# Moving the first head's rough scores, row maxima and shift row into the projection's last tile, with early table loads

## The reference, cut to what matters

```python
u = rmsnorm(h, g_attn)
proj = u @ w_in                      # fox q | k | v | forget logits | MLA q-latent | MLA kv-latent + rope key
fq = rmsnorm(to_heads(fq, 8), g_fox_q); fk = rmsnorm(to_heads(fk, 8), g_fox_k)
cum = cumsum(log_sigmoid(ff + b_f))
logits = (fq @ fk.T) / 8 + cum[query] - cum[key]      # causal, 8 heads of 64 ("fox")
o_fox = softmax(logits) @ fv
# then: MLA (8 heads, low-rank q and kv), output projection, residual,
# and a mixture of 32 experts (top 1 of 4 groups, top 2 of its 8 experts)
```

## Time and profile before

| what | us |
|---|---|
| median of 3 runs | 628.41 (627.26 to 628.76) |
| the profiled execution's own time | 628.14 |
| its span, from the first to the last instruction | 626.4 |
| PE busy | 587.5 (94% of the span) |
| PEld, DVE, ACT, POOL busy | 408.1, 265.6, 233.8, 140.9 |
| mean granted TensorE clock | 0.988 of full speed |

### The profile page before, as it was taken

One profiled execution on the slowest core, in us unless ns is written; L12 is line 12 of the kernel. 1 busy time (PEld: TensorE's weight loads), 2 busy tenths in 40 slices (PEclk: granted clock), 3 DMA queues, 4 the chain that ended last, 5 costly groups with the idle time before them and its releaser, 6 DMA issues.

```text
span 626.4 us, 9256 instructions
## 1 busy us (share of the span) xinstructions
PE 587.5 (94%) x3559; PEld 408.1 (65%) x3559; DVE 265.6 (42%) x603; ACT 233.8 (37%) x445; POOL 140.9 (22%) x233
## 2 busy tenths in 40 slices
PE   8899999998999989999989999999999997877896
PEld 8778788786775447666778766566566554554554
DVE  3644245554484988437745771111111111101217
ACT  6826516543555473456616522212122121111220
POOL 6300001150233412122510011332322322212200
PEclk9999799999999989999989999999999999999999
DMA  8930000006400053000199499999999999999995
GB/s 274 335 121 1 0 2 0 1 2 239 182 1 0 34 235 135 10 1 1 30 427 413 146 412 370 372 397 379 395 393 384 389 398 393 394 395 391 398 378 216
DMA packets 32941, 141.64 MB, mean 226 GB/s; under 512 B 8689, under 2 KB 10785, under 8 KB 19841
## 3 DMA queue, kind: packets, MB, share of 16 engines
q1 hardware_dynamic: 26016, 127.02, 52.3%
q0 software_dynamic: 6304, 11.93, 5.8%
q10 hardware_dynamic: 576, 2.10, 0.8%
HBM read 132.85 MB, written 16.06 MB: 238 GB/s over the span
## 4 chain that ended last, share of the span: by engine, by line
PE 82%; DVE 10%; issue 4%; ACT 3%; POOL 1%; DVEq 0%; ACTq 0%; POOLq 0%
PE ps L2314 18%; PE ps L1953 16%; PE ps L2345 10%; PE ps L2149 6%; PE ps L2272 5%; PE ps L2032 4%; PE ps L2138 3%; PE ps L2087 3%; PE ps L2330 2%; PE ps L2107 2%; PE ps L1917 2%; DVE sums_s L1703 1%; PE ps L1926 1%; DVE x L1864 1%; PE ps L2193 1%
## 5 line engine op out<-in xcount | busy, mean ns | idle before, releaser
L2314 PE MATMUL ps<-w,xt 128*64 128x256 f32 x1024 | 116.6, 380 | 15.3 <-issue 15.0
L2314 PEld LDWEIGHTS ps<-w,xt 128*64 128x64 f32 x1024 | 76.9, 137 | 61.7 <-issue 33.0
L1633 DVE TENSOR_TENSOR xt<-ps,g_ffn_c 128x512 f32<-128x512 f32 x32 | 22.0, 692 | 187.1 <-PE ps L2272 187.1
L2345 PE MATMUL ps<-w,hT 128*64 128x512 f32 x256 | 61.8, 604 | 0.0
L1290 ACT ACTIVATE hsb<-ps,row_scale 128x256 f32<-128x256 f32 x32 | 15.2, 475 | 113.8 <-PE ps L2314 113.8
L917 POOL DMA_INDIRECT xg<-h_rows,idx x30 | 28.8, 960 | 109.0 <-PE ps L2272 108.6
L909 POOL DMA_INDIRECT y_rows<-yh,idy x29 | 29.5, 1016 | 65.3 <-ACT yh L1312 62.4
L2149 PE MATMUL ps<-probT,vals 128*128 128x512 f32 (+4 forms) x160 | 42.7, 411 | 1.0 <-POOL probT L846 1.0
L1714 DVE TENSOR_REDUCE nmax<-ps 128x1 bf16<-128x528 f32 (+1 forms) x64 | 28.0, 502 | 35.9 <-PE ps L2108 35.9
L846 POOL TENSOR_SCALAR_AFFINE_SELECT probT<-probT 128x128 f32<-128x128 f32 (+2 forms) x80 | 21.2, 288 | 83.8 <-ACT probT L1202 82.5
L2272 PEld LDWEIGHTS ps<-ident,xg 64*128 64x128 f32 x256 | 30.2, 200 | 11.6 <-issue 11.5
(11 more groups left out here) (353 smaller groups left out, 1061.8 us busy)
## 6 DMA issues: line engine op xcount, KB each, us to landing
w<-in_w SPq DMA_DIRECT2D x96, 1024.0 KB
x<-in_x SPq DMA_DIRECT2D x8, 512.0 KB, 9.5
y_rows<-zeros POOLq DMA_DIRECT2D x1, 4096.0 KB, 12.3
yg<-y_rows SPq DMA_DIRECT2D x4, 1024.0 KB, 11.0
w_in_v<-in_w_in SPq DMA_DIRECT2D x1, 2048.0 KB, 11.0
w_in_k<-in_w_in SPq DMA_DIRECT2D x1, 2048.0 KB, 16.8
w_in_q<-in_w_in SPq DMA_DIRECT2D x1, 2048.0 KB, 21.6
w_oa<-in_w_o SPq DMA_DIRECT2D x1, 2048.0 KB, 10.2
```

Of the source, the lines that this page charges most:

```text
L2314: ins = pe.matmul(ps[j * slots:(j + 1) * slots, 2 + b, 0:F], xt[b][:, k, :], w13[s][:, j, k, :], start=(k == 0), stop=(k == DK - 1))
L2345: ins = pe.matmul(ps[q * slots:(q + 1) * slots, 6 + b, :], hT[b][:, m, :], w2s[s][:, m, q * 512:(q + 1) * 512], start=(m == 0), stop=(m == ...
```

## The change

1. `max_scores` gets the head as an argument: head 0's rough scores go to PSUM banks 0, 1 and 5 and those of all others to 3, 4 and 5, as before.
2. PE: `score_maxes(0)` stands ahead of the projection of the last unit (ckv, tile 3), behind waits for all turned heads' copies, for `narrowed`, the masks, and the units that held banks 0 and 1. `turn_row(0)` stands ahead of the last turn. The fillers there are 7 in place of 14, in another bank. In `attend(0)` both calls are gone, and so are the 3 + 3 fillers; `attend(1)` keeps its own calls and its 2 fillers.
3. DVE: `row_maxes(0)` stands in the projection's loop, at the last unit but one (ckv, tile 2), behind the copy out of tile 1's turn. `attend(1)` keeps its own call for head 8.
4. ACT: behind `shift_row` of heads 0 and 8 a one-column exp is added, and behind `up_square(0)` a call of `load_root_table`.

```diff
-        def max_scores(i):
+        def max_scores(g, i):
             n = query_keys(i)
+            b0 = 0 if g == 0 else 3
             if i == 3:
-                return pair(3, n)
-            bank, c0 = {2: (4, META), 1: (5, 0), 0: (5, query_keys(1))}[i]
+                return pair(b0, n)
+            bank, c0 = {2: (b0 + 1, META), 1: (5, 0), 0: (5, query_keys(1))}[i]
             return ps[:, bank, c0:c0 + n]
...
                 shift_row(g0)
+                act.activation(junk[:, 0:1], eps_c[:, :], ACT.Exp)
                 for g in range(g0, g0 + H):
...
                     if g == H - 1:
                         up_square(0)
+                        load_root_table()
                         up_root(0)
...
+            def row_maxes(g):
+                for n, i in enumerate(MAX_ORDER):
+                    dve.wait_ge(max_scored, 2 * g + n // 2 + 1)
+                    dve.tensor_reduce(nmax[g % 2][:, i:i + 1], max_scores(g, i), X, ALU.max, negate=True
+                                      ).then_inc(maxed, 1)
...
                 if n >= 1 and units[n - 1] in stage_no and not by_act(units[n - 1]):
                     empty_turn(units[n - 1])
+                if n == len(units) - 2:
+                    row_maxes(0)
...
-                row_maxes(g0)
                 if ph == 1:
+                    row_maxes(g0)
                     add_fox(1)
                 row_maxes(g0 + 1)
...
+            def score_maxes(g):
+                h = g % H
+                for n, i in enumerate(MAX_ORDER):
+                    if h and n in (0, 2):
+                        pe.wait_ge(maxed, NT * (g - 1) + n + 2)
+                    keys, to = query_keys(i), max_scores(g, i)
...
+            def turn_row(g):
+                pe.wait_ge(maxed, NT * (g + 1))
+                if g % H:
+                    pe.wait_ge(row_out, g)
...
             for what, u in steps:
+                if what == "project" and u == units[-1]:
+                    pe.wait_ge(turn_act, sum(by_act(v) for v in turns))
+                    pe.wait_ge(turn_low, sum(by_act(v) for v in turns))
+                    pe.wait_ge(narrowed, sum(by_act(v) for v in turns))
+                    pe.wait_ge(masks_made, 15)
+                    unit_emptied(pe, len(units) - 4)
+                    unit_emptied(pe, len(units) - 3)
+                    score_maxes(0)
...
                 if u == steps[-1][1] and what == "turn":
-                    unit_emptied(pe, len(units) - 4)
-                    keep_warm((len(units) - 4) % 4, 14)
+                    turn_row(0)
+                    unit_emptied(pe, len(units) - 2)
+                    keep_warm((len(units) - 2) % 4, 7)
                 turn(u) if what == "turn" else project(u)
...
-                score_maxes(g0)
                 if ph == 1:
+                    score_maxes(g0)
                     out_project(1, 0, 1)
                 score_maxes(g0 + 1)
-                keep_warm(OUT, 0 if ph else 3)
-                turn_row(g0)
-                keep_warm(OUT, 2 if ph else 3)
                 if ph == 1:
+                    turn_row(g0)
+                    keep_warm(OUT, 2)
                     pe.wait_ge(fox_added, 2)
```

More of the change, by code:

```diff
@@ L1981, in gather @@
                 pe.matmul(dst, side, part[b][:, 0:w], start=True, stop=True).then_inc(projected, 1)
-            for what, u in steps:
+            def score_maxes(g):
[4 more added lines that the diff above has]
+                    keys, to = query_keys(i), max_scores(g, i)
+                    q = qTb[0:depth(g), h, i * P:(i + 1) * P]
+                    for c0 in range(0, keys, 512):
+                        c1 = min(keys, c0 + 512)
+                        m0 = max(c0, keys - P)
+                        pe.matmul(to[:, c0:c1], q, kTb[0:depth(g), h, c0:c1], start=True, stop=False)
+                        ins = pe.matmul(to[:, m0:c1], identb[:, :],
+                                        causal[:, m0 - (keys - P):c1 - (keys - P)], start=False, stop=True)
+                    if n in (1, 3):
+                        ins.then_inc(max_scored, 1)
+            def turn_row(g):
+                pe.wait_ge(maxed, NT * (g + 1))
+                if g % H:
+                    pe.wait_ge(row_out, g)
+                for i in range(NT):
+                    ins = pe.matmul(ps[0:1, ROW, i * P:(i + 1) * P], nmax[g % 2][:, i:i + 1], identb[:, :],
+                                    start=True, stop=True)
+                ins.then_inc(row_turned, 1)
+            for what, u in steps:
+                if what == "project" and u == units[-1]:
[6 more added lines that the diff above has]
+                    score_maxes(0)
                 if what == "spread":
@@ L2093, in attend @@
                 g0 = ph * H
[L2095 to L2121, removed]
                 def score(g):
```

## The result

| what | before | after |
|---|---|---|
| median us (runs) | 627.33 (7; 626.17 to 628.76) | 623.44 (7; 622.70 to 624.56) |
| profiled execution's own time | 628.14 | 622.70 |
| its span | 626.4 | 621.1 |
| mean granted clock | 0.988 | 0.982 |

The ratio is 0.9937, 95% interval 0.9919 to 0.9954: 3.9 us faster, where 3.5 were forecast. Against the 628.41 of the first three runs 624.9 had been forecast; over seven runs the kernel before stands 1.1 us lower. The two profiled executions differ by 5.4 us, more than the medians, and most of this document is about which part of that is the change.

The account below looks back on a forecast made before the run. PE was taken to bound the kernel (82% of the chain), with DMA of weights setting the late end but passing the gain on. Seam -3.72 and root +0.20 gave -3.52, from 628.41 to 624.9 us, range 623.7 to 626.3.

Parts of the forecast that it names:

- The seam: Between projection and fox attention: exact scores start at 150.90 to 150.92 in place of 154.64, 3.72 us less.
- Maxima, row, copy: Head 0's maxima (1.75 us), row (0.31) and ACT's copy (0.58) delay nothing; head 1's row is covered by 0.2 us.
- Tables: Added one-column activations on ACT move no table load; at the root 0.20 us more, perhaps 0.10.
- The sum: Seam and root together: -3.72 + 0.20 = -3.52 us, median 624.9 us.
- Rival (a): With thirteen of twenty fillers gone the clock falls at the seam, costing 1.7 to 3.5 us: 626.6 to 628.4; chance 0.07.
- Rival (b): The clock's fall at the seam lasts into the fox heads: 630.3 us or more; chance 0.03.
- (c): Table loads wait with their activations, so the added ones pull them forward, up to 1.28 - 0.20 gained: 623.6; chance 0.04.
- (d): The gain is lost behind fox attention, as weights' stream or another transfer keeps the end: about 627.5 to 628.6; chance 0.06.

Follow-up runs that it names:

- the move alone: The changed kernel without the added one-column activations; 623.45 us, ratio 0.9931 to the kernel before.
- the trimmed one: The kernel before with 8 fillers for 14 ahead of the last turn and none around head 0's row, nothing moved; 629.49 us, ratio 1.0030.
- the tables alone: The kernel before with only the added one-column activations (exp, root); 627.84 us, ratio 0.9997.
- the delay: The changed kernel with 17 more fillers ahead of the second head's rough scores; 627.41 us, ratio 0.9999 to the kernel before.

## Why the prediction was right

- *The seam.* Forecast 3.72, measured 3.65 along the chain. Rough scores 0.85 for 0.95, the last unit 3.27 for 3.19, the second head's rough scores 7.55 behind the turn of tile 1 for 7.47: the list of waits ahead of `attend(0)`, with a wait more in it, took 0.45 where 0.34 had been read. The last turn was put at 148.61 on the clock of before; it came 6.22 us behind the end of tile 1's turn, which is 148.65.
- *Maxima, row, copy.* As forecast: no one waited for them. The second head's row was the nearest thing to a stop: score(0) ends at 153.58 and the row starts there, 0.06 behind the last maximum (151.77 + 1.75 = 153.52), where 0.2 of cover had been forecast; score(0) took 1.55 and not 1.70.
- *Tables.* Direction right, size halved: 0.09 us on the path and not 0.20. The step that was off is the price of a back-to-back start, taken at the full 202 ns of the earlier trace rows where 0.10 had been named beside it.
- *The sum.* -3.65 + 0.09 gives -3.56. The medians moved by 3.9 with an interval of 2.9 to 5.1, so nothing beyond the sum is shown. The profiled pair differed by 5.3 of span: by the table +1.04 ahead of the seam, -3.76 at it, +0.04 in the heads, +0.09 by the root, -1.05 in the MLA stage, -1.66 behind the last copy. The three that are neither seam nor root go with where each execution happened to meet the low clock; the forecast, made on one trace, had no term for that. In the medians nothing of them can be told.
- *Rival (a), the clock.* It didn't happen, so the 0.07 wasn't tested by the result; the experiments say that the reasoning for so low a chance was too light. It leaned on one trace of before in which a seam with two gaps kept 1.00. That seam was kept by its fillers: with six fewer (8 + 3 + 3) the clock fell in the trace, and by their times in most runs, and the new seam without its seven took 626.72 in the median, 3.3 us more than the move alone on the same chip. The price (half of the low stretch, 1.7 to 3.5 us) was right: 3.03 measured. The Trainium skill, "TensorE: Matmul & The Clock Gate", section "A second HAM failure mode: psum-queue depth-cycling", had said that short idles between groups of matmuls can let the clock swing; the second trace without fillers agrees, at 0.50 behind 4 us in which PE worked 1.5, and the first, with the same work and 1.00, shows that it need not.
- *Rival (b), slower.* The same mechanism did make a kernel slower than before, the trimmed one (+2.2 us, ratio 1.0030): its low stretch was about 10 us and its seam only 0.7 shorter, where the forecast, for a seam 3.5 us shorter, had the break-even at 7 us and a loss of over 0.3% at 10.8. So it was a real rival in kind.
- *Rivals (c) and (d)* fell by the tables alone and by the delay.

## What to carry to other kernels

Work that one phase needs first (here rough scores, maxima and the row of its first head) can often be put among the last steps of the phase ahead, where it needs only banks that are free by then; what it takes there is hidden as long as the last copy of that phase sets the seam. Filler matmuls on the chain are not slack until a timed set of runs says so: replace them by useful matmuls, and don't judge by one trace, since eight of ten runs were slower, at a lower mean clock, of a kernel whose first trace showed it at full. Before a difference of two traces is put down to a change, cut both into stages and read the granted clock of each: here 3.7 us of the stages' differences went with the clock, of either sign.

## What the runs showed of the hardware that was not expected

- The clock's fall is a matter of chance from run to run for the same program: with no fillers two executions took 623.8 and 624.0 us at a mean granted clock of 0.982, the others up to 629.4 at 0.969 to 0.979. The traced low stretch lasted about 7 us and cost 3.03 us.
- What a low stretch costs depends on the stage. It cost 1.05 us in the MLA stage and 1.61 in the output projection. Among the experts, where the DMA share is 1.00, it cost nothing that shows: the tables alone had the clock at 0.50 in 533 to 536, 550 to 553 and 567 to 570 us, the kernel before had 1.00 throughout, and both took 316.0 from the last copy to the end.
- A one-column activation squeezed between a table load and the activation that needs it costs 0.09 us on the path, though its row is 0.20 long.
